# A two-layer decoder step: all engine loops written out, waits compared with constants

## The reference

```python
mod = (c @ w_ada_l + b_ada_l).reshape(c.shape[0], N_MOD, -1)          # nine shifts, scales, gates
f = swiglu(rms_norm(x, g[0]) * (1 + sc1) + sh1, w_gu[0], w_dn[0])
x = x + 0.5 * gt1 * rms_norm(f, g[1])
h = rms_norm(x, g[2]) * (1 + sc2) + sh2
xl, gl, q, k, v, qi, ki, wi = project(h, w_in_l, pos)
xc, new_buf = causal_conv(xl, conv_buf, cw, cb)
hs, hT = rg_lru(xc, h0, wa, ba, wx, bx, lam)
y_att = attn_fn(q, k, v, qi, ki, wi)                                   # top-k keys by an indexer's score
y = jnp.concatenate([y_lru, y_att], axis=-1) @ w_o
x = x + gt2 * rms_norm(y, g[3])
f = swiglu(rms_norm(x, g[4]) * (1 + sc3) + sh3, w_gu[1], w_dn[1])
x = x + 0.5 * gt3 * rms_norm(f, g[5])
```

## Time and profile before

| | |
|---|---|
| median of 3 runs | 3291.97 us (3281.11 to 3292.07) |
| profiled execution: span from first to last instruction | 3289.0 us |
| taken as its own time (span and what lies around it) | about 3292 us: the median less the span leaves 3.0 us |
| PE busy, PEld busy | 2866.4 us (87%), 2643.8 us (80%) |
| DVE, ACT, POOL busy | 1465.7 us (45%), 782.9 us (24%), 158.8 us (5%) |
| mean granted TensorE clock | 0.886 |
| instructions of all kinds | 56073 |

### The profile page before, as it was taken

How to read it: one execution, slowest core, us unless ns; L and a number is a source line. 1 busy time by engine, 2 the same in 40 slices (tenths; PEclk the granted TensorE clock), 3 DMA queues, 4 the chain that set the end, 5 groups by cost and what they waited for, 6 DMA issues and landing times.

```text
span 3289.0 us, 56073 instructions
## 1 busy us (share of the span) xinstructions
PE 2866.4 (87%) x20506; PEld 2643.8 (80%) x20506; DVE 1465.7 (45%) x2006; ACT 782.9 (24%) x1076; POOL 158.8 (5%) x299
## 2 busy tenths in 40 slices
PE   5999997987778669999979999969796768699997
PEld 4999896976545669999969998969575548699997
DVE  2333124365799443332243331244648983533312
ACT  2233023220012133332223321222200122333221
POOL 0000001001320000000000000010113100000000
PEclk8999998975579789999989999989656888899998
DMA  6223632212353012322243226222123421123231
GB/s 183 82 85 89 176 88 79 73 43 61 112 148 109 26 39 83 89 85 74 87 123 89 84 82 186 85 72 75 48 69 110 146 86 40 42 85 89 69 88 62
DMA packets 524666, 291.09 MB, mean 89 GB/s; under 512 B 20673, under 2 KB 518882, under 8 KB 524162
## 3 DMA queue, kind: packets, MB, share of 16 engines
q1 hardware_dynamic: 513154, 266.35, 27.9%
q0 software_dynamic: 11392, 23.23, 2.4%
HBM read 285.75 MB, written 3.77 MB: 88 GB/s over the span
## 4 chain that ended last, share of the span: by engine, by line
PE 78%; DVE 7%; issue 6%; SPq 3%; DMA 2%; ACT 2%; DVEq 0%; POOL 0%; ACTq 0%; POOLq 0%
PE ps L581 19%; PE ps L583 19%; PE ps L582 19%; PE ps L703 4%; PE ps L592 4%; PE ps L553 3%; PE ps L701 3%; DMA sb_wslot<-w_ada 2%; PE ps L819 2%; SPq L433 2%; SPq L431 1%; PE ps L563 1%; ACT sb_h L864 1%; PE ps L723 1%; DVE sb_h L1149 1%
## 5 line engine op out<-in xcount | busy, mean ns | idle before, releaser
L582 PE MATMUL ps<-sb_h_lo,sb_w_hi 128*128 128x272 f32 x3360 | 974.4, 290 | 0.0
L581 PE MATMUL ps<-sb_h_hi,sb_w_hi 128*128 128x272 f32 x2816 | 818.7, 291 | 54.3 <-DVE sb_h_lo L1135 54.3
L583 PE MATMUL ps<-sb_h_hi,sb_w_lo_ffn 128*128 128x272 f32 x2816 | 820.8, 291 | 0.0
L874 ACT ACTIVATE sb_w_hi<-sb_wslot 128x1024 fp32r<-128x1024 f32 (+2 forms) x322 | 332.9, 1036 | 1485.9 <-PE ps L583 1337.0
L1110 DVE TENSOR_TENSOR sb_w_lo_ffn<-sb_wslot,sb_w_hi 128x1024 fp32r<-128x1024 f32 (+1 forms) x272 | 324.0, 1194 | 794.6 <-ACT sb_w_hi L874 794.0
L582 PEld LDWEIGHTS ps<-sb_h_lo,sb_w_hi 128*128 128x128 f32 x3360 | 642.3, 191 | 0.5
L581 PEld LDWEIGHTS ps<-sb_h_hi,sb_w_hi 128*128 128x128 f32 x2816 | 535.1, 190 | 59.4 <-issue 54.2
L583 PEld LDWEIGHTS ps<-sb_h_hi,sb_w_lo_ffn 128*128 128x128 f32 x2816 | 534.5, 190 | 0.0
L581 PE MATMUL ps<-sb_act_hi,sb_w_hi 128*128 128x272 f32 x1408 | 408.7, 290 | 11.1 <-DVE sb_w_lo_ffn L1110 11.1
L583 PE MATMUL ps<-sb_act_hi,sb_w_lo_ffn 128*128 128x272 f32 x1408 | 407.6, 290 | 0.0
L582 PE MATMUL ps<-sb_act_lo,sb_w_hi 128*128 128x272 f32 x1408 | 407.3, 289 | 0.0
(11 more groups left out here) (218 smaller groups left out, 3199.7 us busy)
## 6 DMA issues: line engine op xcount, KB each, us to landing
sb_wslot<-ffn_w_gu SPq DMA_DIRECT2D x176, 512.0 KB, 3.7
sb_wslot<-w_ada SPq DMA_DIRECT2D x144, 512.0 KB, 4.7
sb_wslot<-ffn_w_down SPq DMA_DIRECT2D x64, 512.0 KB, 3.9
sb_wslot<-w_in SPq DMA_DIRECT2D x32, 512.0 KB, 3.7
sb_wslot<-ffn_w_down SPq DMA_DIRECT2D x32, 384.0 KB, 3.4
sb_down<-key_pages POOLq DMA_DIRECT2D x128, 96.0 KB, 2.2
sb_down<-key_pages SPq DMA_DIRECT2D x128, 96.0 KB, 2.0
sb_wslot<-w_out SPq DMA_DIRECT2D x16, 512.0 KB, 3.9
```

Of the source, the lines that this page charges most:

```text
L581: mm(out, wh, xh, start=(kc == 0), stop=False)
L582: mm(out, wh, xl, start=False, stop=False)
L583: last = mm(out, wl, xh, start=False, stop=(kc == of - 1))
L874: act_fn(w_hi[s][:, 0:rows, 0:cols], wslot[i][:, 0:rows, 0:cols], ACT.Copy).then_inc(w_hi_done.sem, 1)
```

## The change

`PAGE_UNROLL`, `hold`, its semaphores and `Steps.loop` go. Every `Fori` becomes a loop of Python, so that each engine's program is written out for both layers, all rounds and all pages; the layer, the round and the pair are then numbers, and so is the value of every wait and the address of every transfer, save the page number, which is still read from `sb_pages`. What `hold` waited for, a plain wait waits for. Order and contents of the work are the same. The core of the diff:

```diff
-def hold(eng, passed, sem, value):
-    eng.wait_ge(sem, value)
-    eng.sem_inc(passed, 1)
...
     def need(self, n):
-        self.eng.wait_ge(self.sem, self.layer * self.per + (n + self.shift))
-
-    def need_hold(self, n):
-
-        hold(self.eng, self.passed, self.sem, self.layer * self.per + (n + self.shift))
+        self.eng.wait_ge(self.sem, self.layer * self.per + n)
...
         def load_pages(eng, tensor, l, seq_page, first, after, buf, full):
-            with eng.Fori(0, (after - first) // PAGE_UNROLL) as j:
-                for n in range(PAGE_UNROLL):
-                    k = j * PAGE_UNROLL + (first + n)
-                    load_page(eng, tensor, l, seq_page + k, buf[:, bass.ds(k, 1), :], full)
+            for k in range(first, after):
+                load_page(eng, tensor, l, seq_page + k, buf[:, bass.ds(k, 1), :], full)
...
             for i in range(2):
-                hold(eng, who, kp_used[i].sem, kp_used[i].at(l, pair))
+                eng.wait_ge(kp_used[i].sem, kp_used[i].at(l, pair))
...
-            with sp.Fori(0, DEPTH) as l:
+            for l in range(DEPTH):
...
-                    hold(sp, passed[0], ada_used[i].sem, ada_used[i].at(l, before[0]))
+                    sp.wait_ge(ada_used[i].sem, ada_used[i].at(l, before[0]))
                     sp.wait_ge(w_split[i].sem, w_split[i].at(l, before[1]))
...
-                with pe.Fori(first, after) as g:
+                for g in range(first, after):
                     for m in range(DC):
                         ada_chunk(l, ph, g * RPF + (-first * RPF), m, m // RING)
...
-                with pe.Fori(0, U_GU) as u:
+                for u in range(0, U_GU):
...
-                hold(pe, passed[1], relu_ready.sem, relu_ready.at(l, len(DOTS)))
-                with pe.Fori(1, NSEQ // 2) as pair:
+                pe.wait_ge(relu_ready.sem, relu_ready.at(l, len(DOTS)))
+                for pair in range(1, NSEQ // 2):
                     page_products(pair)
...
-            with dve.Fori(0, DEPTH) as l:
-                st = Steps(dve, dve_step, DVE_STEPS, l, passed[3])
+            for l in range(DEPTH):
+                st = Steps(dve, dve_step, DVE_STEPS, l)
...
-                    st.need_hold(found)
+                    st.need(found)
                     replaced = st.mark(v.match_replace(scS, top_s, scS, TAKEN))
```

More of the change, by code:

```diff
@@ L12 @@
-from contextlib import ExitStack, contextmanager
+from contextlib import ExitStack
 import numpy as np
@@ L479, in pieces @@
                 def pieces(ph, src, first=0, start=0, rounds=None):
-                    with sp.Fori(start, start + (rounds or ph.rounds)) as u:
+                    for u in range(start, start + (rounds or ph.rounds)):
                         for n in range(RING):
@@ L493, in ffn_loads @@
                     between()
-                    with sp.Fori(0, DC // 2) as u:
+                    for u in range(0, DC // 2):
                         for n in range(2 * len(DN_K)):
@@ L611, in ada @@
                     ada_transposes(l, g, 2)
-                hold(pe, passed[1], ada_read.sem, ada_read.at(l, after))
+                pe.wait_ge(ada_read.sem, ada_read.at(l, after))
             def ffn(l, f, gu_ph, dn_ph, between):
-                with pe.Fori(0, U_GU) as u:
+                for u in range(0, U_GU):
                     for n in range(RING):
@@ L654, in swapped @@
                     product(2 + n % 2, [swap], [proj[:, c, :]]).then_inc(sw_ready.sem, 1)
-                with pe.Fori(0, QQ // RING) as u:
+                for u in range(0, QQ // RING):
                     for n in range(RING):
@@ L824, in _ @@
                 for half in range(2):
-                    hold(pe, passed[1], pv_copied.sem, pv_copied.at(l, half + 1))
+                    pe.wait_ge(pv_copied.sem, pv_copied.at(l, half + 1))
                     for s in range(half * 4, half * 4 + 4):
@@ L832, in _ @@
                 pe.wait_ge(ada_read.sem, ada_read.at(l, NMOD))
-                hold(pe, passed[1], y_parts.sem, y_parts.at(l, 1))
-                with pe.Fori(0, DC // RING) as u:
+                pe.wait_ge(y_parts.sem, y_parts.at(l, 1))
+                for u in range(0, DC // RING):
                     for n in range(RING):
@@ L880, in in_rounds @@
             def in_rounds(ph, body, peeled=1):
-                with sc.Fori(0, ph.rounds - peeled) as u:
+                for u in range(0, ph.rounds - peeled):
                     body(u, lambda n: True)
@@ L925, in _ @@
             sc.wait_ge(eps_ready.sem, 1)
-            with sc.Fori(0, DEPTH) as l:
+            for l in range(DEPTH):
                 l_[0] = l
@@ L988, in _ @@
                         .then_inc(relu_ready.sem, 1)
-                with sc.Fori(1, NSEQ // 2) as pair:
+                for pair in range(1, NSEQ // 2):
                     page_scores(pair)
@@ L1061, in _ @@
             pool.wait_ge(s_in.sem, 64)
-            with pool.Fori(0, DEPTH) as l:
+            for l in range(DEPTH):
                 key_loads(pool, False, l, 0)
@@ L1066, in _ @@
                     .then_inc(states_stored.sem, 16)
-                with pool.Fori(1, 2) as pair:
+                for pair in range(1, 2):
                     key_loads(pool, False, l, pair)
@@ L1071, in _ @@
                     .then_inc(states_stored.sem, 16)
-                with pool.Fori(2, NSEQ // 2) as pair:
+                for pair in range(2, NSEQ // 2):
                     key_loads(pool, False, l, pair)
-                hold(pool, passed[2], arena_free.sem, arena_free.at(l, 1))
+                pool.wait_ge(arena_free.sem, arena_free.at(l, 1))
                 for s in range(V_POOL):
                     load_pages(pool, a["v_cache"], l, s * PAGES, 0, PAGES, vpage[s], vp_full[s])
-                hold(pool, passed[2], max_in.sem, max_in.at(l, 1))
+                pool.wait_ge(max_in.sem, max_in.at(l, 1))
                 nc.gpsimd.partition_all_reduce(mxa, mx, P, RMAX).then_inc(pool_max.sem, 1)
@@ L1181, in gate_up @@
                                 .then_inc(act_ready.sem, 1)
-                    with st.loop(U_GU - 1, 2) as u:
+                    for u in range(U_GU - 1):
                         gate_up(u, lambda n: True)
@@ L1188, in ffn_operands @@
                         split(dn_ph, 0, n, w_lo_ffn)
-                    with dve.Fori(0, dn_ph.rounds - 1) as u:
+                    for u in range(0, dn_ph.rounds - 1):
                         for n in range(dn_ph.per_round):
@@ L1209, in ada @@
                 def ada(ph, first, after):
-                    with dve.Fori(first, after) as g:
+                    for g in range(first, after):
                         for half in range(2):
@@ L1304, in conv_tap @@
                         last.then_inc(conv_done.sem, 1)
-                with dve.Fori(0, QQ // RING) as u:
+                for u in range(0, QQ // RING):
                     for n in range(RING):
@@ L1453, in _ @@
                 in_loop = ROUNDS // (NSEQ // 2 - 1)
-                with st.loop(NSEQ // 2 - 1, 6 * in_loop, start=1) as pair:
+                for pair in range(1, NSEQ // 2):
                     for i in range(2):
```

66 lines of the change are left out of this document (25 added, 41 removed).

## The result

The changed kernel takes 3244.14 us (3242.64 to 3247.34, four runs) against 3290.28 us of the kernel before on the same chip: a ratio of 0.9868, with a 95% interval of 0.9851 to 0.9884, so 38 to 49 us off. The forecast was 30.3 us off. Most of the time came from the forecast places, but they gave more than the sum, and more than its upper bounds together (38.2 us).

The account below looks back on a forecast made before the run. The chain lies mostly on FFN products, which loops do not delay; control reaches it in the attention, layer turn, page products and conditioning. Sum 5.2 + 16 + 2.7 + 1.4 + 3 + 2 = 30.3 us off 3292.0: 3262 us, range 3246 to 3286.

Parts of the forecast that it names:

- A: DVE's turn from layer 0 to layer 1: removing the branch saves 5.2 us, once; bounds 4.7 to 5.2.
- B: SP's value pages in the attention: 1.13 us a page instead of 1.40 closes DVE's waits, 16 us; bounds 8.4 to 17.5.
- F: DVE's attention steps: 0.09 us of register arithmetic goes from each of 64, taken as 2 us; bounds 0 to 5.8.
- C: POOL's key pages: earlier issue removes PE's idle time before page products, 2.7 us over two layers; bounds 0 to 2.7.
- D: PE's control before the first page products: 0.7 us a layer saved, 1.4 us in all; bounds 0 to 2.0.
- E: Conditioning rounds: PE's turns between groups and SP's control before each piece, 3 us; bounds 0 to 5.
- What was costed at nothing: Loops of IN, OUT, GU and DN on SP, PE and DVE: 0 us, hidden by queued matmuls.
- the value pages that give back little: Rival: removed instructions on SP's value pages ran beside others, gain 8.4 us or less, time near 3279 us; chance 0.15.
- The slower straight code: Rival: PE stands still for 152 more instruction packets, 122 us slower, 3384 us; chance 0.08.
- The larger gain: Rival: PE's idle time before L581 shrinks by a third as DVE comes sooner, 18 us more, 3244 us; chance 0.05.

Follow-up runs that it names:

- the kernel with that loop alone: Kernel before, with only DVE's loop over the layers written out, inner loops and holds kept: 3282.39 us, ratio 0.9980.
- the value pages alone: Kernel before, with only the loop over SP's value pages written out: 3269.94 us, ratio 0.9954.
- a slower page: The changed kernel, with the page number of SP's value pages read twice: 3271.12 us against 3240.84 of the change on the same chip.
- DVE alone: Kernel before, with all of DVE's program written out and the other engines keeping their loops: 3272.42 us, ratio 0.9947.
- PE alone: Kernel before, with only PE's program written out: 3282.74 us, ratio 0.9981.
- POOL alone: Kernel before, with only POOL's program written out: 3282.81 us, ratio 0.9978.
- SP alone: Kernel before, with only SP's program written out: 3276.83 us against 3289.70, ratio 0.9958.
- SP and POOL: Kernel before, with SP's and POOL's programs written out and the others keeping their loops: 3267.64 us, ratio 0.9940.
- all but PE: The changed kernel with PE's old program, so PE alone keeps its loops: 3246.32 us, ratio 0.9882 against the kernel before.

## Why the prediction was right, and what it undersized

The range held, with little to spare. The 43 us are beyond the 38.2 us of all upper bounds together (3254 us), and 3248.5 us lies inside the range only by the 8 us that I had added below for the scatter of the runs; the second measurement of the change, at a ratio of 0.9860, would be at 3245.9 us, right at its edge.

**A** was 5.2 us: 5.5 in the trace, 3 to 11 us by the kernel with that loop alone. **B**, 16 us at 1.13 us a page: the page measured 1.14, the value pages alone gave 17.6 us of attention and 15 us in all, and a slower page brought the waits back. With **F** (2 us) I had 18 us for the attention; the change has 21.5. F is near its upper bound: most steps got 0.11 to 0.13 us shorter, those in which DVE also copies conditioning did not, and together that is about 5 us. Once B had closed the waits, nothing took its place, which I had held as likely as not. Without B it is taken back (DVE alone: 1.3 us).

**C and D**, 4.1 us, gave 7.6. D was sized as one stop of 0.7 us a layer; the stop vanished whole, 0.99 to 0.04. PE alone shows 6.7 us in this stage: PE's holds and addresses stood before the first product of each pair of sequences, and I had put the 0.84 and 0.49 us of the earlier trace rows down to late pages only. Either an earlier page or a shorter start closes such a stop: with POOL alone neither of the two is left, with PE alone 0.26 us at one.

**E**, 3 us with 5 as its upper bound, stands against 7.8 in the table, but that row is not conditioning alone. Its 32 products for the sums of squares in layer 0, before and then in the change:

```profile
52.67:63.26 10.59, 9.28 (x32) 7.05 (x32) 2.83 (x5) 3.05 (x3) 0.00 (x0) 0.84 0.64 184
```

```profile
50.37:59.05 8.68, 7.60 (x32) 6.00 (x32) 2.83 (x5) 2.96 (x3) 0.00 (x0) 1.00 0.72 203
```

This stretch gave 1.9 us, with the granted clock at 0.84 and then at 1.00; at 1.00 both times, layer 1 gave 0.2. The first copy of layer 0 came 0.9 us sooner. The ten rounds themselves gave 4.8 us, and 4.1 in the second run: within E's bounds, and 1 to 2 us above what I took, since I had priced each round's control by itself. The chain at ADA1 of layer 0, before:

```profile
346.49 3.60 PE ps L592 x32
...
350.48 5.00 DMA sb_wslot<-w_ada
355.51 3.66 PE ps L592 x32
359.21 1.93 PE ps L592 x16
```

and now:

```profile
341.49 14.14 PE ps L560 x128
355.65 0.69 DVE sb_modT L1166
...
356.80 14.24 PE ps L560 x128
```

Before, the chain went by turns through products and a landing of 5 us; now PE's 128 products of a group are one stretch of it for two groups, and a landing comes back in the third. PE had work from other slots during most of such a landing: over the three groups it idled 3.1 us before and 1.5 now. Transfers and products were nearly level, with PE busy for 45.7 of 49.0 us before and the DMA engines for 0.84 of that time, so I take it that the control in between decided which of them set the pace. Which engine's control counts is not shown: the ten rounds gave 1.0 us with SP alone, 0.6 with DVE alone, nothing with PE or POOL alone, 2.8 with SP and POOL, 2.4 with all but PE, and they took 2.6 us longer in the kernel of the value pages, which leaves them as they were.

What was costed at nothing came to 1 us in the change and 6.7 us in its second run: the FFNs' loops, OUT, IN and DN, with the idle time of the earlier trace rows unmoved in the change. What the sum had no term for is the clock: PE's busy time fell by 6.8 us in the change, 12.3 us in its second run, for the same products. With DVE alone it fell by 12.8, about as much as the 11 us beside the turn there; all four executions of that kernel had a mean granted clock of 0.888 or 0.889, against 0.883 to 0.887 in the 19 of before beside them. Whether the one is the other, and why the clock was better in those runs, stays open.

Of the rivals, the value pages that give back little fell with the first page at 1.14 us. The slower straight code fell with PE alone: 97 more instruction packets, and 3 to 9 us less time. The Trainium skill ("Runtime: NRT & Kernel Launch", section Instruction fetch mechanics) has it so: running on into the next block is mostly hidden, a taken branch to a target that is not held stops the engine for a fetch. The runs agree with both, 161 packets without a price that shows and a stop of 4.5 to 4.7 us at the one far branch on the path; that this stop is a fetch, no run here shows. The larger gain was nearer than I gave it (3244 us, chance 0.05), but not by its mechanism: DVE did not come sooner before L581.

## What to carry to other kernels

Look for loops on an engine where its sequencer, and not its unit, is what others wait for: a queue of small transfers, the turn of a long loop, the wait before a stage's first product. Price the control of one such item (here 1.40 against 1.14 us) and see whose slack it has used up; a loop whose unit has work queued is worth nothing to write out. When one engine's issuing gets faster, ask what its next transfers will overtake.

## What was not expected of the hardware

A branch back over a long program stopped DVE for 4.67 and 4.52 us, nearly the same for two lengths of the loop, while PE's branches of a GU round take 76 to 220 ns. Conditioning pieces issued ahead of POOL's last pages on another queue raised the landing of the last one to 5.7 us, where 2.2 is the median. And two executions of one program differed by 11.7 us, with a granted clock of 0.54 in one and 1.00 in the other at the same place.
